# RWKV-7 head passes: TensorE's projection piece ahead of the next group's inverse level in every chunk, instead of behind it

## The reference

```python
def rwkv_scan(r, w, k, v, kk, a, S0):
    def step(S, inp):
        r_t, w_t, k_t, v_t, kk_t, a_t = inp
        sa = jnp.einsum('bhvk,bhk->bhv', S, -kk_t)
        S = (S * w_t[:, :, None, :] + sa[..., None] * (kk_t * a_t)[:, :, None, :]
             + v_t[..., None] * k_t[:, :, None, :])
        return S, jnp.einsum('bhvk,bhk->bhv', S, r_t)
```

## Time and profile before

| | us |
|---|---|
| median of three runs | 3780.89 |
| lowest and highest | 3779.38, 3785.51 |
| the profiled execution | 3783.18 |
| its span in the trace | 3781.4 |
| the head passes in it (119.2 to 709.4) | 590.2 |

### The profile page before, as it was taken

How to read it: one execution, slowest core, us unless ns; L and a number is a source line. 1 busy time by engine, 2 the same in 40 slices (tenths; PEclk the granted TensorE clock), 3 DMA queues, 4 the chain that set the end, 5 groups by cost and what they waited for, 6 DMA issues and landing times. The chain is left out here.

```text
span 3781.4 us, 62512 instructions
## 1 busy us (share of the span) xinstructions
PE 3468.6 (92%) x26131; PEld 2878.9 (76%) x26131; DVE 1470.8 (39%) x2710; ACT 833.5 (22%) x1582; POOL 560.1 (15%) x384
## 2 busy tenths in 40 slices
PE   8888887898878869999999998999988999999996
PEld 5566665554446559999999995666648999999996
DVE  4465666423366663323232233332323332222321
ACT  2233221111256522111111112222213211111110
POOL 0000000103000004222222221000003322222221
PEclk9899898899799979999999999999998999999998
DMA  2000000303200041111111103011123111111112
GB/s 101 19 21 8 25 7 14 120 29 79 78 1 1 7 158 49 45 45 44 43 50 33 45 28 118 23 61 51 40 93 111 52 49 40 49 34 45 50 34 102
DMA packets 73474, 189.21 MB, mean 50 GB/s; under 512 B 26916, under 2 KB 41188, under 8 KB 70132
## 3 DMA queue, kind: packets, MB, share of 16 engines
q1 hardware_dynamic: 59956, 156.92, 12.2%
q0 software_dynamic: 8960, 28.32, 2.3%
q10 hardware_dynamic: 4352, 1.05, 0.1%
HBM read 161.34 MB, written 29.04 MB: 50 GB/s over the span
## 5 line engine op out<-in xcount | busy, mean ns | idle before, releaser
L177 PE MATMUL ps<-ff_x,ff_wh 128*128 128x384 f32 (+1 forms) x3960 | 774.9, 328 | 0.0
L177 PEld LDWEIGHTS ps<-ff_x,ff_wh 128*128 128x128 f32 x3960 | 668.8, 188 | 0.8
L177 PE MATMUL ps<-ff_x,ff_wl 128*128 128x384 f32 (+1 forms) x2112 | 465.5, 328 | 0.0
L177 PEld LDWEIGHTS ps<-ff_x,ff_wl 128*128 128x128 f32 x2112 | 360.8, 188 | 0.0
L520 DVE TENSOR_TENSOR resid<-resid,ps 128x384 f32 (+1 forms) x240 | 113.2, 527 | 386.7 <-PE ps L177 386.7
L2536 PE MATMUL ps<-act,gl_w 128*128 128x384 f32 (+1 forms) x768 | 244.6, 474 | 0.0
L177 PE MATMUL ps<-ff_hh,ff_dh 128*128 128x384 f32 (+1 forms) x1056 | 233.4, 329 | 7.1 <-DVE ff_hl L512 4.6
L177 PE MATMUL ps<-ff_hh,ff_dl 128*128 128x384 f32 (+1 forms) x1056 | 232.7, 328 | 0.0
L177 PE MATMUL ps<-ff_hl,ff_dh 128*128 128x384 f32 (+1 forms) x1056 | 232.7, 328 | 0.0
L2536 PEld LDWEIGHTS ps<-act,gl_w 128*128 128x128 f32 x768 | 144.4, 192 | 90.3 <-issue 10.6
L507 DVE TENSOR_TENSOR ff_prod<-ff_silu,ps 128x384 f32<-128x384 f32 x132 | 62.3, 527 | 349.6 <-PE ps L177 349.6
(11 more groups left out here) (603 smaller groups left out, 5457.6 us busy)
## 6 DMA issues: line engine op xcount, KB each, us to landing
ff_w<-in_wg SPq DMA_DIRECT2D x44, 512.0 KB, 3.4
ff_w<-in_wu SPq DMA_DIRECT2D x44, 512.0 KB, 3.5
ff_wd<-in_wd POOLq DMA_DIRECT2D x48, 256.0 KB, 3.0
ff_wd<-in_wd POOLq DMA_DIRECT2D x32, 320.0 KB, 3.3
rw_w<-in_w_rwkv SPq DMA_DIRECT2D x14, 512.0 KB, 3.5
ns_past<-in_cache_slc SPq DMA_DIRECT2D x48, 128.0 KB, 2.2
np_w<-in_w_nsa SPq DMA_DIRECT2D x8, 652.0 KB, 8.1
resid<-in_x SPq DMA_DIRECT2D x1, 4352.0 KB
```

The lines of the kernel that those rows point to most:

```text
L177: mm = pe.matmul(g.ps[:, bank + c, 0:n], w[:, k, :], x[:, o:o + n], start=(first and i == 0), stop=(last and i == 2))
```

## The change

In every chunk of groups 0 to 3, in all four passes, TensorE's even piece `beside(j, 8 * i + 2 * c)` changes places with `inverse(j, i + 1, 2 * c)`, the even level of the next group. The odd level and the odd piece keep their places. DVE, ACT, POOL and SP keep their programs word for word; no instruction is added or removed.

```diff
                     for c in range(4):
                         through(j, i, c)
+                        beside(j, 8 * i + 2 * c)
                         inverse(j, i + 1, 2 * c)
-                        beside(j, 8 * i + 2 * c)
                         update(j, i, c)
                         inverse(j, i + 1, 2 * c + 1)
                         beside(j, 8 * i + 2 * c + 1)
```

## The result

| | us |
|---|---|
| before, median of four runs | 3781.44 (3779.38 to 3785.51) |
| after, median of four runs | 3809.9 (3807.46 to 3812.06) |
| ratio | 1.0074, 95% interval 1.0062 to 1.0086 |
| span of the profiled execution | 3808.0, before 3781.4 |

The change makes the kernel slower by 28 us. The forecast was 3796 with a range of 3785 to 3808: the sign was right, the size was half of what came, and the time lies outside the range.

The account below looks back on a forecast made before the run. PE was taken to set the pace in the head passes, with about 100 us of waits for DVE or ACT. Eight terms summed to +14.5 us on 3780.9, giving 3795.4, said as 3796; range 3785 to 3808.

Parts of the forecast that it names:

- Term 1: Passes 0 to 2, groups 0 and 1: piece 0 or 8 fills the mask wait of 1.96 us; -11.5 us.
- term 2: Passes 0 to 2, chunks 0 to 2 of four-chunk groups: 22 new waits of 0.58 us behind `update`; +12.8 us.
- term 3: Piece 16, three passes: it needs `kk0` taken and doesn't fit into the mask wait; +2.4 us.
- 4, piece 12: Piece 12, passes 1 and 2: the chain through DVE's reciprocal starts 2.13 us later, all on the path; +4.3 us.
- term 5: Piece 18, passes 1 and 2: DVE's own step of 1.28 us delays its copy of level 3; +1.2 us.
- 6, piece 30: Piece 30, passes 0 and 1: level 6 stands behind an ACT wait and the piece, delaying the state; +3.0 us.
- 7, single pieces of pass 3: Pass 3, pieces 3 and 4, 9 and 10: single matmuls in one bank wait for it to be taken; +1.8 us.
- term 8: Piece 24: short mask waits could be covered, against DVE's own piece and bank waits; +0.5 us, bounds -3.2 and +3.
- the four chains: Chains through DVE and ACT at pieces 16, 12, 18 and 30: +2.4, +4.3, +1.2 and +3.0 us.
- the step on the clock: Granted clock in the head passes: taken as 0 us, bounds -3 and +8.
- The clock suffers: Rival: one in three of 22 new waits brings a half-clock stretch of some 1.4 us; +25, 3805 us; chance 0.14.

Follow-up runs that it names:

- experiment 5: After, plus two unread 128x128 matmuls behind `update` where the level waited (27 places), one ACT wait moved; 3813.94 us against before's 3783.57, ratio 1.0076.
- experiment 1: Before with only pieces 0 and 8 of passes 0 to 2 ahead of their level; 3775.26 us against 3782.09, ratio 0.9984.
- experiment 3: After with pieces 16 and 30 (all passes) and 12 and 18 (from pass 1) in the old order; 3781.87 us against before's 3782.09, ratio 1.0000.
- experiment 2: After with chunk 0 of every group in the old order; 3821.02 us against before's 3782.09, ratio 1.01.
- experiment 8: Four kernels, each before with part of the change: ten plain places 1.0029, last four pieces of groups 3 1.0028, pieces 12 and 18 1.0003, piece 16 1.0023.
- 7: The kernel of experiment 1 with one projection matmul of pieces 1 and 9 moved between level 0 and `update`; 3771.98 us against before's 3783.57, ratio 0.9972.
- only12_18: Before with only pieces 12 and 18 of passes 1 and 2 ahead of their level; 3785.52 us, ratio 1.0003.
- 4: Before with even and odd pieces ahead of their levels in groups 0 and 1, passes 0 to 2, ahead of the reciprocal; 3783.75 us against 3782.09, ratio 1.0002.

## Why the prediction was right in sign and half in size

The measured column is the sum of the steps of after that are no clock, taken where two kernels have the same clock in the chunk. The spans differ by 26.6 where 14.5 was forecast; of the 12.1 that are missing the clock is 6.1, and the rest is nearly all in terms 1, 2, 5 and 8.

| term | predicted | measured |
|---|---|---|
| 1, six covered waits, with their share of term 2 | -11.5 + 3.5 | 3 x -1.39 - 0.63 - 2 x 1.17 = -7.1 |
| 2, the ten plain places | 10 x 0.58 = 5.8 | 10 x 0.80 = 8.0 |
| 3, piece 16, with its handovers | 4.1 | 3 x 1.38 = 4.1 (read at equal clock in passes 0 and 2) |
| 4, piece 12 | 4.3 | 2 x 2.29 = 4.6 |
| 5, piece 18, with its handovers | 2.9 | 1.23 + 2 x 1.39 = 4.0 |
| 6, piece 30 | 3.0 | 1.39, taken twice = 2.8 (read in pass 0) |
| 7, single pieces of pass 3 | 1.8 | 1.9 |
| 8, group 3 | 0.5 | 2.2 |
| sum | 14.5 | 20.5 |
| the clock | 0 | 6.1 |

(The row for the handovers is split as term 2 counted them: 22 places of 0.58 are six in row 1, ten in row 2, three each in rows 3 and 5.) The 6.1 is what is left of the 26.6 between the spans; the parts that the clock makes longer or shorter give 6.7 if added one by one, and the first copy of `u` comes 0.6 earlier. The chunks of piece 20 (steps of 0.24, 0.79 and 0.94) are counted as clock: every kernel here has a stretch at the lower clock in them, so what the new order does there was not read apart from it.

**Right.** The covered waits, the four chains and pass 3, each by its named mechanism. That term 3 fits to the tenth is partly luck: its own times give 374.3 - 373.1 = 1.2 a pass, not 1.3, and less the 0.58 that is 0.6, not 0.8, so that the term with its handovers would have been 3.6. Piece 16 waits for DVE's take of `kk0`:

```profile
380.25 0.55 DVE L2323 TENSOR_SCALAR rw_e<-ps 128x384 f32<-128x384 f32 x1
...
380.85 1.32 PE L1907 MATMUL ps<-rw_e,const 128*128 128x384 f32 x2 [2.43 <-DVE rw_e L2323]
```

The first reciprocal is reached later: level 5 waits for the handover, the piece follows, and `through` waits 4.63 where it waited 3.15. With the wait of 0.58 in front and the broken row that is 1.48 + 0.58 + 0.23 = 2.3. At the second reciprocal the wait is 3.29 where it was 2.86, and ahead of piece 30 ACT is waited for 1.01 instead of 0.73:

```profile
359.34 0.46 PE L1825 MATMUL ps<-rw_up,rw_lowi 64*64 64x64 f32 x16 [0.58 <-DVE rw_lowi L2222]
359.73 2.20 PE L1899 MATMUL ps<-act,rw_w 128*128 128x384 f32 x6
366.56 0.48 PE L1842 MATMUL ps<-rw_wg,rw_up 64*64 64x64 f32 x4 [4.63 <-DVE rw_st L2257]
...
403.02 0.48 PE L1870 MATMUL ps<-rw_u,rw_tok 64*64 64x64 f32 x4 [3.29 <-DVE rw_u L2240]
...
434.44 1.38 PE L1907 MATMUL ps<-rw_lora,rw_lw 64*128 64x320 f32 x4 [1.01 <-ACT rw_logw L2092]
```

**Wrong: the step on the clock.** "By the rows short waits don't pull it down. I take 0." Nothing contradicts the first sentence (experiment 5, and the plain chunks below). The second doesn't follow from it: that the short waits leave the clock alone says nothing on what the new order does to it. Time at the lower clock rose from 122.9 to 146.2 us and cost 6.1 us. The rival *The clock suffers* was nearest with its 3805, but its mechanism, a stretch at every third new wait, is not what the trace shows: no plain chunk with a new wait lost its full clock. The largest single piece is the end of pass 0 (+4.0), which has no new wait in it; others are chunks in which group 4's state or piece 16 is waited for (+1.4 to +1.8), and some places gained (-1.63 where pass 0's half-clock piece 8 ran at full clock, and as much at the first chunk of pass 2).

**Wrong: 0.58 as the price of a new break.** Term 2 priced the wait and not the small matmuls around it: 2.2 us in its ten places, and the same 0.2 sits in term 5 (1.39 for 1.18 in passes 1 and 2). In pass 0 piece 18 costs 1.23 for 0.58, for there DVE also waits 0.35 for ACT's copy ahead of the reciprocal. Before's trace had the 0.23 in it: `through` with its level takes 1.07 there. I read the wait in pass 3 and never added up a whole chunk in both orders. Term 1 doesn't have it, since the wait for the masks had broken the row there already: 1.96 covered less 0.57 gives -1.39 in group 0, as forecast. What term 1 misses is in group 1, above all in pass 0 (-0.63 for -1.30), where DVE's own piece 8 stands ahead of its copy of `u`, so that `update` waits (0.59 in experiment 1's trace).

**Mis-sized: term 8.** It was "not read to the end", taken as 0.5 within -3.2 and 3. The short mask waits gave 0.25 (passes 1, 2) and 0.6 (pass 3), but chunk 1 of group 3 steps by 0.57 to 0.95, in every pass: 2.2 in all. The reason that the term gave, a DVE nearly without idle time, is what sets it: PE now does level 2 behind piece 26, and DVE, which had copied it at once, stands idle for it, 0.80 in pass 1 and 0.43 in pass 0; its long steps behind the copy, and with them the next copy of `u`, come later. The prediction had the direction of this wait open and gave it no price; in pass 0 part of it is paid only together with piece 30 (experiment 3).

**What stays open.** Why the clock falls in one kernel and not in another at the same instructions. Experiment 5 speaks against the short waits, and experiment 2 shows that the wait for the masks sometimes brings a stretch at the lower clock and sometimes doesn't: in three of nine such places of before. Shifting the whole program in time without changing the order was not tried.

## What to carry to other kernels

Between two dependent steps on an in-order engine, a piece of independent work is worth the handover that it hides; moving it to an earlier wait pays only where that wait is longer than the handover which it leaves open. So move it where the wait is long (six of the 64 places here gave 7.1 us, and the others next to nothing) and cut off a small part to leave behind, rather than change the order everywhere. Price a moved piece by what it leaves uncovered, by the runs of small instructions that it breaks, and by the buffers that the work between two pieces gave time to empty.

A kernel whose clock goes between two levels needs a comparison by steps at fixed places of the trace: by the time alone experiment 8 would have called 7.4 us of real waits free, and experiment 3 would have called 5.6 us free, with the ten plain places' 8.0 among them.

## What the runs showed of the hardware

The pattern of the granted clock is repeatable and at the same time not local. Two executions of before agreed in it in every chunk (122.9 us of lower clock both times), while every edit moved it (us of lower clock in the passes): 108.6 us in experiment 3, 119.1 in 7, 122.9 in 1, 122.9 in `only12_18` and 133.1 to 141.9 in the other three of experiment 8's kernels, 124.9 in 4, 153.6 in 2, 157.0 in 5; where the sum stayed, the places moved. Untouched code 50 us behind an edit ran 3 us slower at a clock of 0.77 instead of 0.90. With the steps outside the clock taken off, the clock was worth between -9 us (experiment 3) and +14 (experiment 2, where they make 25 of 39), as much as the whole change. One kernel (only piece 16 moved) spread over 15 us in its own ten runs.
